# A transformer block pair on one core: where the second lane of the chunked recurrence begins, and what stands behind its triangular solve

## The reference, cut to what matters

```python
def step(state, inp):
    r_t, w_t, k_t, v_t, kk_t, a_t = inp
    sa = jnp.einsum('bhvk,bhk->bhv', state, -kk_t)
    state = (state * w_t[:, :, None, :]
             + sa[..., None] * (kk_t * a_t)[:, :, None, :]
             + v_t[..., None] * k_t[:, :, None, :])
    return state, jnp.einsum('bhvk,bhk->bhv', state, r_t)
...
mean = jnp.mean(y, axis=-1, keepdims=True)
var = jnp.mean(jnp.square(y - mean), axis=-1, keepdims=True)
y = ((y - mean) * lax.rsqrt(var + GN_EPS)).reshape(B, S, RWKV_WIDTH) * ln_w + ln_b
bonus = jnp.sum(r * k * r_k, axis=-1, keepdims=True) * v
y = y + bonus.reshape(B, S, RWKV_WIDTH)
return (y * g).astype(p_r.dtype)
```

## Time and profile before

| | us |
|---|---|
| median of 3 runs | 1494.02 (1493.59 to 1494.42) |
| the profiled execution, its own time | 1492.87 |
| its span in the trace | 1491.1 |
| PE busy in the span | 1439.0 (97%) |
| POOL, DVE, ACT busy | 778.8, 544.7, 497.7 |
| the mix: first `tV` to the first output product | 969.96 to 1072.75 |

### The profile page before, as it was taken

One profiled execution on the slowest core, in us unless ns is written; L12 is line 12 of the kernel. 1 busy time (PEld: TensorE's weight loads), 2 busy tenths in 40 slices (PEclk: granted clock), 3 DMA queues, 4 the chain that ended last, 5 costly groups with the idle time before them and its releaser, 6 DMA issues.

```text
span 1491.1 us, 21683 instructions
## 1 busy us (share of the span) xinstructions
PE 1439.0 (97%) x8056; PEld 1193.3 (80%) x8056; DVE 544.7 (37%) x755; ACT 497.7 (33%) x683; POOL 778.8 (52%) x1026
## 2 busy tenths in 40 slices
PE   7998999999999999999999999968899999999997
PEld 5877888888888788888888878767687888888887
DVE  6985422222003832222100568954535222221003
ACT  6433433333113332222211485123433323222112
POOL 1662745545555855554555657361455555545553
PEclk9898999999999999999999999989999999999999
DMA  9772432223322323223322222100122232323221
GB/s 362 306 315 85 141 113 98 98 98 98 99 98 72 102 96 105 92 98 98 99 99 95 76 77 80 57 2 3 49 94 99 85 109 87 98 98 99 98 71 57
DMA packets 45705, 156.96 MB, mean 105 GB/s; under 512 B 5328, under 2 KB 8656, under 8 KB 45520
## 3 DMA queue, kind: packets, MB, share of 16 engines
q1 hardware_dynamic: 45648, 156.16, 30.5%
HBM read 154.04 MB, written 2.10 MB: 105 GB/s over the span
## 4 chain that ended last, share of the span: by engine, by line
PE 84%; DVE 9%; issue 3%; ACT 2%; POOL 1%; DMA 0%; DVEq 0%; SPq 0%; POOLq 0%; ACTq 0%
PE ps L1733 26%; PE ps L1734 26%; PE ps L1735 26%; PE ps L2154 2%; DVE tri_p L1154 1%; DVE tri_x L1154 1%; POOL w_lo L524 1%; DVE mid_sq L1157 1%; DVE act_lo L1157 0%; DVE mod_acc L1157 0%; DVE pads L1154 0%; PE ps L2106 0%; DVE rAR L1157 0%; DVE rB L1154 0%; DVE f_buf L1154 0%
## 5 line engine op out<-in xcount | busy, mean ns | idle before, releaser
L524 POOL TENSOR_TENSOR w_lo<-raw,w_hi 128x256 fp32r<-128x256 f32 x932 | 696.1, 781 | 585.2 <-ACT w_hi L703 585.0
L1733 PE MATMUL ps<-act_hi,w_hi 128*128 128x512 f32 x1328 | 524.7, 395 | 4.1 <-DVE act_lo L1157 2.6
L1735 PE MATMUL ps<-act_hi,w_lo 128*128 128x512 f32 x1328 | 519.0, 391 | 0.0
L1734 PE MATMUL ps<-act_lo,w_hi 128*128 128x512 f32 x1328 | 518.9, 391 | 0.0
L703 ACT ACTIVATE w_hi<-raw 128x1024 fp32r<-128x1024 f32 x233 | 244.8, 1054 | 435.1 <-PE ps L1735 404.8
L1733 PEld LDWEIGHTS ps<-act_hi,w_hi 128*128 128x128 f32 x1328 | 250.8, 189 | 60.5 <-issue 4.9
L1734 PEld LDWEIGHTS ps<-act_lo,w_hi 128*128 128x128 f32 x1328 | 250.6, 189 | 52.9 <-issue 1.9
L1735 PEld LDWEIGHTS ps<-act_hi,w_lo 128*128 128x128 f32 x1328 | 250.5, 189 | 52.7
L1733 PE MATMUL ps<-hid_hi,w_hi 128*128 (+2 forms) x588 | 220.3, 375 | 2.9 <-DVE hid_lo L1154 2.1
L1734 PE MATMUL ps<-hid_lo,w_hi 128*128 (+2 forms) x588 | 220.1, 374 | 0.0
L1735 PE MATMUL ps<-hid_hi,w_lo 128*128 (+2 forms) x588 | 220.1, 374 | 0.0
(11 more groups left out here) (278 smaller groups left out, 1009.8 us busy)
## 6 DMA issues: line engine op xcount, KB each, us to landing
raw<-weight_units SPq DMA_DIRECT2D x233, 512.0 KB, 3.5
wm_mid<-mod_units SPq DMA_DIRECT2D x18, 512.0 KB, 8.4
wm_ring<-mod_units SPq DMA_DIRECT2D x14, 512.0 KB, 8.6
wm_early<-mod_units SPq DMA_DIRECT2D x8, 512.0 KB, 7.8
wm_late<-mod_units SPq DMA_DIRECT2D x8, 512.0 KB, 7.8
x_tok<-tokens SPq DMA_DIRECT2D x4, 512.0 KB, 6.5
xT<-tokens_by_channel SPq DMA_DIRECT2D x1, 2048.0 KB, 8.5
result<-act_out SPq DMA_DIRECT2D x16, 128.0 KB, 1.8
```

The costliest lines, as they stand in the source:

```text
L524: ins = nc.gpsimd.tensor_tensor(w_lo[:, slot, c], raw[:, slot, c], w_hi[:, slot, c].bitcast(f32), SUB)
L1733: nc.tensor.matmul(o, wh, xh, start=start, stop=False, **check)
L1734: nc.tensor.matmul(o, wh, xl, start=False, stop=False, **check)
L1735: return nc.tensor.matmul(o, wl, xh, start=False, stop=stop, **check)
```

## The change

- `in_turns` now advances only the even lane, by 4 segments, and takes turns from there. The odd lane stands 4 segments behind the even one instead of 7, and 4 segments of it are left for `closing` to alternate with instead of 7. Pair 1's masks are thereby behind the solve and behind pair 0's `G1`.
- On DVE, `bonus(0)` and `bonus(1)` move from ahead of the solve's last steps to behind it, `bonus(2)` and `bonus(3)` from pair 0's segment 0 to the end of its segment 3.
- Of pair 0's four factor blocks ACT copies two and DVE the other two, right behind the solve. ACT's copies are made by `copy` instead of `activation` with the same function.
- POOL's pooling waits for `tri_done`; so that this can't hold up pair 1's `X`, the wait for that step is taken for every pair.
- `cent` is computed by POOL in two instructions behind the statistics of the second feed-forward layer, in a part of `sumsq`, instead of by one of DVE in the solve.

```diff
--- before.py
+++ after.py
@@ -188,10 +188,9 @@
     return pair // 2 * len(steps) + steps.index(name) + 1
 
 
-LAG = 7
 BEFORE_MIX = 3
 LOW_FIRST = 5
-AHEAD_OF_SOLVE = 3
+AHEAD_OF_SOLVE = 4
 SOLVED = 29
 
 
@@ -204,10 +203,7 @@
             yield from pair_program(p)
 
     even, odd, after_even = lane(0), lane(1), closing()
-    for first in (even, odd):
-        for _ in range(AHEAD_OF_SOLVE):
-            next(first)
-    for _ in range(LAG):
+    for _ in range(AHEAD_OF_SOLVE):
         next(even)
     for _ in even:
         next(odd)
@@ -354,7 +350,7 @@
         tri_p = view("tri_p", [P, SB * SB // 4], o_tb)
         off = view("off", [P, PAIRS * NSYS, SB], o_acc)
 
-        cent = view("cent", [P, P], o_tb + 2 * T)[:, :]
+        cent = sumsq[:, P:2 * P]
 
         def half_set(n, **places):
 
@@ -371,6 +367,11 @@
                 half_set(1, AA=o_whi + 6 * t4, G1=o_whi + 2 * t4, MBR=o_whi, VT=o_whi + t4, MT=o_whi + 4 * t4, MK=o_wlo, GH=o_wlo + 2 * t4,
                          RP=o_wlo + 4 * t4, BT=o_wlo + 6 * t4, KT=o_wlo + 7 * t4, TT=o_hid + 37 * t4, X=o_hid + 39 * t4, S=o_hid + 41 * t4)]
         masks = sumsq[:, 0:2 * CH].rearrange("p (k t) -> p k t", t=CH)
+
+        def triangle_block(copy, p, e):
+
+            r = slice(e * SB, (e + 1) * SB)
+            copy(sets[p % 2].TT[r, :, e % 2 * SB:(e % 2 + 1) * SB].rearrange("q (h c) t -> q h c t", h=2), systems_of(tri_t, p)[r]).then_inc(sem("tri_blocks"), 1)
 
         def over_chunks(tile, n):
 
@@ -603,6 +604,10 @@
                 nc.gpsimd.memset(t[:, :, :], 0.0).then_inc(sem("cleared"), 1)
 
 
+            pool.wait_ge(sem("stat"), turn_of("f1"))
+            nc.gpsimd.tensor_scalar(cent, bones, -1.0 / HS, None, MUL, ALU.bypass).then_inc(sem("centre"), 1)
+            pool.wait_ge(sem("centre"), 1)
+            nc.gpsimd.tensor_tensor(cent, cent, ident, ADD).then_inc(sem("centre"), 1)
             pool.wait_ge(sem("bc_mm"), PAIRS)
             n_chain[0] += 1
             nc.gpsimd.memset(tri_x[:, :, :], 0.0).then_inc(sem("pool_chain"), 1)
@@ -649,8 +654,9 @@
                     if e == 0:
                         ins.then_inc(sem("half_made"), 1)
                 did("X", ins)
+                po_did("X")
                 if p == 1:
-                    po_did("X")
+                    pool.wait_ge(sem("tri_done"), 1)
                     pool.wait_ge(sem("in_read"), len(IN_ORDER))
                     for b_ in (pool_b, pool_c):
                         n_chain[0] += 1
@@ -995,10 +1001,8 @@
                 act.wait_ge(sem("cleared"), cleared_through(f"TT{p % 2}"))
                 if p >= 2:
                     act.wait_ge(tensor_step[p % 2], at(PE_STEPS, p - 2, "GH"))
-                for e in range(4):
-                    r = slice(e * SB, (e + 1) * SB)
-                    ins = nc.scalar.activation(b.TT[r, :, e % 2 * SB:(e % 2 + 1) * SB].rearrange("q (h c) t -> q h c t", h=2), systems_of(tri_t, p)[r], ACT.Copy)
-                    ins.then_inc(sem("tri_blocks"), 1)
+                for e in range(2 if p == 0 else 4):
+                    triangle_block(nc.scalar.copy, p, e)
 
             def pair(p):
                 pe_did, ve_did, ac_did, po_did = step_waits(act, p)
@@ -1489,7 +1493,6 @@
                 chain(nc.vector.transpose(tri_m[:, :, :], tri_g[:, :, :].rearrange("p n t -> p t n")))
                 after(sem("tri_unit"), 1)
                 after(sem("g_mm"), PAIRS)
-                stt(cent, bones, -1.0 / HS, ident, MUL, ADD, "centre")
                 yield
                 for u in range(SB - 1):
                     n_t, n_s = SB - 1 - u, u + 1
@@ -1552,8 +1555,6 @@
                 if i == 16:
                     solve_steps(3)
 
-            bonus(0)
-            bonus(1)
             solve_steps(1)
             after(unit_used, U_OUT)
             after(sem("loaded_masks"), 32)
@@ -1580,9 +1581,6 @@
                     did(name, nc.vector.tensor_tensor(
                         b.MK[:, g, :, :, :], ps[:, b.bank + 2:b.bank + 4, :].rearrange("q h (c g t) -> q h c g t", c=NCP, g=2)[:, :, :, g, :],
                         over_chunks(masks[:, g, :], NCP), MUL))
-                if p == 0:
-                    bonus(2)
-                    bonus(3)
                 yield
                 pe_did("LR")
                 did("LR", nc.vector.tensor_tensor(b.MBR[:, :, :, :], by_half(0, 0), over_chunks(masks[:, 1, :], NCP), MUL))
@@ -1592,11 +1590,20 @@
                 if p == 0:
                     solve_steps(SB - 1 - SOLVED)
                     solve_steps(1)
-                yield
+                    after(sem("cleared"), cleared_through("TT0"))
+                    for e in (2, 3):
+                        triangle_block(nc.vector.tensor_copy, p, e)
+                yield
+                if p == 0:
+                    bonus(0)
+                    bonus(1)
                 pe_did("G1")
                 did("G1b", nc.vector.tensor_copy(b.G1[:, 2:4, :, :], bank(1).rearrange("q (c h t) -> q c h t", c=2, h=2)))
                 pe_did("tK")
                 did("tK", nc.vector.tensor_copy(b.KT[:, :], bank(3)))
+                if p == 0:
+                    bonus(2)
+                    bonus(3)
                 yield
                 pe_did("W")
                 did("Wb", nc.vector.tensor_copy(b.W[:, 2:4, :, :], bank(3).rearrange("q (c h t) -> q c h t", c=2, h=2)))
@@ -2115,7 +2122,7 @@
                     pe.wait_ge(vector_step[p % 2], at(VE_STEPS, p - 2, "y"))
                 elif p == 1:
                     after(sem("prep"), 2)
-                after(sem("centre"), 1)
+                after(sem("centre"), 2)
                 for c in range(NCP):
                     cols = slice(c * P, (c + 1) * P)
                     last = nc.tensor.matmul(bank(0)[:, cols], rV[:, p, cols], cent, start=True, stop=True)
```

## The result

| | before | after |
|---|---|---|
| median, us | 1494.22 (1493.59 to 1494.59, 4 runs) | 1503.50 (1502.26 to 1504.48, 4 runs) |
| the profiled execution, its own time | 1492.87 | 1503.97 |
| its span | 1491.1 | 1502.2 |
| first `tV` to the first output product | 102.79 | 114.80 |
| PE idle in it | 21.37 | 23.74 |

A forecast was written before the change was run, and what follows sets the result against it. PE bounds the kernel, so only its idle time and slow clock count: 6.5 us more idle, plus 2.1 at the start and 4.5 for new falls, less 4.8 before, gave 8.3 slower: 1502.3 us, range 1496.5 to 1507.

The forecast's parts named there:

- The start: Up to pair 1's `G1`: pair 0's `G1` 6.5 us sooner, PE idle 8.4 us against 11.1.
- The idle time behind it: Waits behind pair 1's `G1` and in the tail; with the start, 30.9 us idle against 24.3, 6.5 more.
- the addition: Engine segments laid end to end with 0.15 us gaps; said to overstate waits by some 3 us in either order.
- 27 to 31 us idle: Sign expected in the profile after: PE's idle time between the first `tV` and the first output product.
- under 15 behind pair 1's `G1`: Sign that would prove the prediction wrong: PE idle less than 15 us behind pair 1's `G1`.
- The clock: Slow-clock loss in the mix: 2.1 us at the start and 4.5 for new falls, against 4.8 before.
- The four falls: Clock falls at the ends of pairs 0, 1 and 2 and in the tail, 4.5 us together.
- The quarter taken off: Discount on the new clock falls, 6.0 to 4.5 us, for slow work lying where PE would have waited.
- (1): Whole mix: early start holds, other waits hide behind one another, `var` and `bc` under 0.4 us each; 1490 us, 6%.
- (2): Solve's end: POOL's pooling collides with DVE's block copies, `G1` 1 us later, clock lower still; 1504 us, 6%.
- (3): Middle of the mix: clock holds, 3.8 us slower, last fall 1.7 at most; 1498 to 1499 us, 16%.
- (4): Pairs 1 and 3: clock stays low through most of them, 2 or 3 more falls; 1507 us, 10%.

The follow-up runs named there:

- e9: Changed kernel with the lanes 8 segments apart, and DVE also copying two of pair 1's four factor blocks: 1488.06 us, ratio 0.9959 to the kernel before.
- e13: Changed kernel with two extra unread 256-column products ahead of each `var` and `bc` of the first three pairs: 1498.52 us, ratio 1.0034 to the kernel before.
- e1: Changed kernel with the even lane 7 segments ahead instead of 4: 1492.87 us, ratio 0.9998 to the kernel before.
- e4: Changed kernel with one extra unread 256-column product ahead of each `var` and `bc` of the first three pairs: 1500.48 us, ratio 1.0059 to the kernel before.
- e11: Changed kernel with the even lane 7 segments ahead and ACT alone copying all four of pair 0's blocks: 1493.88 us, ratio 1.0005 to the kernel before.
- e7: Kernel before with one part of the change alone, POOL's pooling waiting for the solve: 1491.03 us, ratio 0.9986 to the kernel before.
- e6: Changed kernel with ACT's first three weight roundings of the tail moved ahead of the last pair's square: 1500.36 us, ratio 1.0054 to the kernel before.

## Why the prediction was right, and where it was not

**The start: right.** `G1` at 979.59 (979.8 said), released by ACT's copy; `G1` of pair 1 released by ACT's `TT`, though with 0.20 us of wait and not 1.3. Up to it 8.4 us of idle time were said and 23.7 - 16.5 = 7.3 measured (PE is busy for 70.09 of the 86.54 us from 998.21 on). DVE's copy, for which no row stood, is 0.3 each, near the 0.25 taken, and hidden.

**The idle time behind it: mis-sized.** The term was 6.5 us more; 2.4 were measured. `var` and `bc` of pair 0 wait 1.08 and 0.98 (1.4 and 1.3 said), `S6` 0.71 (1.0), the last `bc` 2.46 (3.5), the last `var` not at all (0.8). In part the gaps between engines are shorter than the 0.15 us that the addition gave to each: ACT's square of pair 0 ends at 1015.09 + 0.63 = 1015.72, and `var` begins at 1015.77. In part the slow matmuls stood where waits would have been: the last `Y` and two pooling products behind it took 1.81 and 2.00, and `rK` was ready when `var` came. "27 to 31 us idle" was wrong (23.7); "under 15 behind pair 1's `G1`" was not reached (16.5).

**The clock: right in place, too small by far.** The four falls are where the prediction put them. It priced all four at 4.5 us, from the single fall of the tail before (1.7), less a discount for slow work that lies where PE would have waited. They cost about 2.9 each. That is the mis-sized term: the one before had cost 1.7 in 3.4 us at the lower level, and these last 6.8 us each. The quarter taken off for slow work in place of waiting is no cheaper fall in the trace: the slow matmuls took their time in full, and what they hid shows as less idle time. With the start, +8.9 us measured against +1.8 in the sum. The two errors stand against each other (4.1 too much, 7.1 too little) and leave 11.1 us between the profiled executions for the 8.3 forecast. So the time came out close partly by luck.

**The rivals.** That the early start holds (1) is refuted, though the `var` and `bc` waits are a quarter smaller than I had them. That pooling collides with DVE's copies (2) didn't happen: 0.61 for two, and POOL's first long step began at 979.63, behind them. In e9, where two such copies do meet a pooling step, they took 1.15. That the clock holds in the middle (3) is refuted by the windows, and e13 comes near to what it would have been like. Of (4), a clock low through whole pairs, there is nothing: it came back after 6.8 us each time.

## What to carry to other kernels

Two chains that run in turns should be set apart by the distance at which the hand-over waits of the one, here copy, square and root at a pair's end, meet dense products of the other; try one step more and one less before anything else, since it is one number (here 4, 7 and 8 gave 1.0071, 0.9998 and 0.9962). Waits of 1 us can cost more than 1 us each: read the granted clock in windows of 2 us beside every chain of narrow products, and price a fall by how long it lasts. Don't judge by one fall in one trace; compare the mean granted clock of all executions. The early start of pair 0 gave nothing that could be measured here, since the wait ahead of it had been filled with work that now came later.

## What the runs showed of the hardware

- Between 968 and 1098 us the fourteen traces have 31 falls of TensorE's clock. Nineteen last 6.8 us, also the one at 1018.5, in which PE is busy without a gap from 1019.85 on. Six last 3.4 us (in before and e1 the one at 1073), five 10.2 (the start in before) and one 13.7 (the end of e4). What decides between them is open, and near-identical kernels fall at different places (e11 at 1005, e7 at 1064.6); e6 has no fall at 1029, where the kernel after has one behind the same instructions.
- Work that nobody needs made the kernel 0.37% faster, by keeping the clock up (e13 against the kernel after; granted clock 0.984 to 0.986 against 0.979 and 0.980).
- A DVE product of 31 elements with both inputs in SBUF took 1.06 us beside GpSimd's pooling step and 0.19 without it; e7 turns this on and off alone. The Trainium skill (SBUF — State Buffer, section SBUF: two separate sides) describes the cause, a pair of ports that one of the two engines holds for a whole instruction; the trace agrees, since the 1.06 us ended with GpSimd's 1.04 us step. A DVE copy of 32x256, from SBUF to SBUF, took 0.30 us in the kernel after and 0.57 beside GpSimd's 1.29 us step (e9).
